# Token-major weight products in pairs of 512 columns, and attention, recurrence and latent attention in another order of work

## The reference, cut to what matters

```python
# first block, twice
h = rms_norm(x, attn_norm[i]);  proj = h @ w_in[i]              # 1024 -> 2304 (q, k, v) + 3072 (gates)
qa, ka, va, qb, kb, vb, qc, kc, vc, gates = jnp.split(proj, SPLIT_POINTS, axis=-1)
# per head: rms_norm and rope on q, k; softmax attention (full, window 128 with sinks, differential)
g = jax.nn.sigmoid(gates.reshape(B, S, N_BRANCH, D))
merged = g[:, :, 0] * (ya @ w_pa[i]) + g[:, :, 1] * (yb @ w_pb[i]) + g[:, :, 2] * (yc @ w_pc[i])
x = x + merged @ w_out[i]
u = causal_depthwise_conv(rms_norm(x, mlp_norm[i]) @ w_up[i], conv_w[i], conv_b[i])
x = x + (jax.nn.silu(gate_u) * val_u) @ w_down[i]
...
# recurrence (LRU) of the second block
gate_branch, rec = jnp.split(x @ w_in, 2, axis=-1);  u = causal conv of rec (4 taps) + conv_b
r = sigmoid(u_blocks @ w_a + b_a);  i = sigmoid(u_blocks @ w_x + b_x)
log_a = -8 * r * softplus(-lam);  a = exp(log_a)
b_in = sqrt(-expm1(2 * log_a)) * (i * u);  h_t = a_t h_{t-1} + b_in_t
return (h * gelu(gate_branch)) @ w_o
...
# latent attention (MLA) of the second block
c_q, c_kv, k_pe = jnp.split(x @ w_in, [384, 640], axis=-1)
q = rms_norm_2(c_q, q_norm_g) @ w_uq;  kv = rms_norm_2(c_kv, kv_norm_g) @ w_ukv   # rope on parts, softmax, @ w_o
...
# every MLP of the second block
return jnp.square(jax.nn.relu(x @ w1)) @ w2
```

## Time and profile before

| | us |
|---|---|
| median of 3 runs | 2251.13 |
| lowest, highest | 2250.94, 2255.55 |
| the profiled execution | 2252.48 |
| its span in the trace | 2250.7 |
| PE busy | 2151.1 (96% of the span) |
| DVE, ACT, POOL busy | 1391.1 (62%), 1097.8 (49%), 142.2 (6%) |
| share of PE's granted clock, mean | 0.989 |
| HBM read | 374.87 MB, 167 GB/s over the span |

### The profile page before, as it was taken

The page is one execution under the profiler, slowest core; times in us unless marked ns, Lnnn a source line. Parts: engine busy times, 40 slices in busy tenths (PEclk is TensorE's granted clock), DMA queues, the critical chain, the costliest instruction groups (busy, mean ns, idle before and its releaser), DMA issues.

```text
span 2250.7 us, 33710 instructions
## 1 busy us (share of the span) xinstructions
PE 2151.1 (96%) x14705; PEld 1979.4 (88%) x14711; DVE 1391.1 (62%) x1473; ACT 1097.8 (49%) x1262; POOL 142.2 (6%) x82
## 2 busy tenths in 40 slices
PE   6998999998899999999999989998999999999998
PEld 6888899898889999988999878997789989988997
DVE  4856677676567766656655685555666557465654
ACT  4475555555636554344544574443545434354443
POOL 1100010020001002300000010000000004000000
PEclk9999999999999999999999999999999999999999
DMA  7433555563245555644556545565345565545553
GB/s 234 155 103 126 171 185 184 170 203 111 80 164 173 187 186 170 199 131 158 191 189 209 176 131 169 188 202 159 122 139 186 188 205 177 175 150 170 186 188 130
DMA packets 272268, 378.10 MB, mean 168 GB/s; under 512 B 13957, under 2 KB 234362, under 8 KB 272122
## 3 DMA queue, kind: packets, MB, share of 16 engines
q1 hardware_dynamic: 271212, 374.57, 51.1%
q10 hardware_dynamic: 910, 1.38, 0.2%
HBM read 374.87 MB, written 1.05 MB: 167 GB/s over the span
## 4 chain that ended last, share of the span: by engine, by line
PE 81%; DVE 7%; ACT 4%; DMA 2%; DVEq 2%; issue 1%; SPq 1%; PEld 0%; POOL 0%; ACTq 0%; PEldq 0%; POOLq 0%
PE bank L682 51%; PE acc L682 28%; DVE slot_lo L1725 3%; PE bank L680 2%; DVEq L1720 2%; ACT slot_hi L1323 1%; DMA slot<-in_w_in 1%; DMA slot<-in_lru_w_in 1%; ACT arena L1318 1%; SPq L557 0%; PEld bank L682 0%; DVE arena L2279 0%; DVE split L1758 0%; ACT split L1351 0%; DVE arena L2064 0%
## 5 line engine op out<-in xcount | busy, mean ns | idle before, releaser
L1725 DVE TENSOR_TENSOR slot_lo<-slot,slot_hi 128x2048 fp32r<-128x2048 f32 (+1 forms) x344 | 806.9, 2350 | 422.6 <-ACT slot_hi L1323 421.4
L682 PE MATMUL bank<-split,slot_hi 128*128 128x256 f32 x5496 | 1004.3, 285 | 9.6 <-DVE slot_lo L1725 3.4
L682 PEld LDWEIGHTS bank<-split,slot_hi 128*128 128x128 f32 x5496 | 865.4, 193 | 23.4 <-issue 10.4
L1323 ACT ACTIVATE slot_hi<-slot 128x2048 fp32r<-128x2048 f32 (+1 forms) x344 | 652.9, 1902 | 280.8 <-DMA slot<-in_mlp_w 137.3
L682 PE MATMUL bank<-split,slot_lo 128*128 128x256 f32 x2748 | 779.8, 284 | 0.0
L682 PE MATMUL acc<-slot_hi,split 128*128 128x512 f32 x1904 | 610.4, 393 | 13.7 <-DVE split L2318 8.4
L682 PEld LDWEIGHTS bank<-split,slot_lo 128*128 128x128 f32 x2748 | 529.2, 193 | 0.0
L682 PEld LDWEIGHTS acc<-slot_hi,split 128*128 128x128 f32 x1904 | 359.8, 189 | 91.9 <-DVE split L2318 8.6
L682 PE MATMUL acc<-slot_lo,split 128*128 128x512 f32 x952 | 373.2, 392 | 0.0
L682 PE MATMUL bank<-slot_hi,split 128*128 128x256 f32 (+1 forms) x1616 | 306.4, 289 | 21.4 <-DVE split L1758 11.8
L1318 ACT ACTIVATE arena<-bank 128x512 f32<-128x512 f32 (+1 forms) x199 | 111.6, 573 | 388.2 <-PE bank L682 358.2
(11 more groups left out here) (195 smaller groups left out, 1036.5 us busy)
## 6 DMA issues: line engine op xcount, KB each, us to landing
slot<-in_mlp_w SPq DMA_DIRECT2D x128, 1024.0 KB, 5.4
slot<-in_ret_w_in SPq DMA_DIRECT2D x48, 1024.0 KB, 5.2
slot<-in_w_up SPq DMA_DIRECT2D x44, 1024.0 KB, 5.1
slot<-in_w_in SPq DMA_DIRECT2D x42, 1024.0 KB, 5.4
slot<-in_w_down SPq DMA_DIRECT2D x22, 1024.0 KB, 4.9
slot<-in_ret_w_o SPq DMA_DIRECT2D x16, 1024.0 KB, 4.9
slot<-in_lru_w_in SPq DMA_DIRECT2D x10, 1024.0 KB, 7.8
slot<-in_w_out SPq DMA_DIRECT2D x8, 1024.0 KB, 6.1
```

Source lines behind the costliest of these rows:

```text
L682: i = nc.tensor.matmul(o, w, m, start=start, stop=stop)
L1323: A(whi[u.r][:, 0:u.cols], raw[u.r][:, 0:u.cols], ACT.Copy).then_inc(slot_hi[u.r], 1)
L1725: TTO(wlo[u.r][:, 0:u.cols], raw[u.r][:, 0:u.cols], f32(whi[u.r][:, 0:u.cols]), ALU.subtract)\
```

## The change

Slots and products:

- Where two token-major chunks of 256 columns stood, there is now a pair: two slots, each with half of the contraction (512 rows) and 512 columns, and two banks, one for each token tile. A pair is 2 x 24 matmuls of 512 columns where there were 2 x 48 of 256. There are 23 pairs: 4 in each layer's q, k, v (`PAIRS` takes the place of `CHUNKS`), the head of the up projection in each layer, the heads of the four MLPs and of the recurrence, and four in each retention. Chunk 5 stays single.
- In a head, `rows_come` issues the matmuls that need only the high part of the activations for a half of the features, 8 for each half and token tile, then those that need the low part. Before, `token_rows` waited for the low part first, and the three products of each tile stood together.

Layers of the first block:

- Gate chunks 0, 1 and 2 stand ahead of the transposes of q and k (before: 0 and 1), gate 3 behind them, gate 4 between the first two groups of scores, then 5.
- The values of a head wait for that head's copy of the probabilities, not for those of all heads of the group.
- DVE's `divisors(3)` stands ahead of `scores(4)`.
- `yt` 3 is transposed one branch earlier, and its low part made one earlier.

Recurrence: chunk 2 is done first and chunks 0 and 1 are brought back behind it; gates 0 to 5, chunk 5, gates 6 to 9; the groups are six and four feature tiles; the sigmoid is written as a tanh of half the argument, its halves folded into the constants; POOL's product and ACT's square move to DVE; each group's output has its own `lyT` tile.

Latent attention: the layer norm rows are issued behind `mukv`; ACT copies the first two banks ahead of the high parts of `muq` 0 and 1; DVE makes the low part of `mukv` 1 ahead of the first `exchanged` of q.

The rows of the other norms (`gain`, `layer_norm`) are issued in the middle of the stages, at s = 5 or 8, or behind the first output slot of a retention.

```diff
-CHUNKS = (6, 7, 0, 1, 3, 5, 4, 2, 8)
+PAIRS = ((6, 7), (0, 1), (3, 4), (5,), (2, 8))
+LRU_ORDER = (2, 0, 1, 3, 4)
+LRU_GROUPS = (slice(0, 6), slice(6, 10))
...
+            def rows_come(u, o, name, tt, i, end):
+
+                w = [part[u.r][:, :].rearrange("p (k n) -> p k n", n=512) for part in (whi, wlo)]
+                h = [part[:, 4 * i:4 * i + 4, tt * P:(tt + 1) * P] for part in hT]
+                pe.wait_ge(V["hi_out"], his[name, (tt, i)].uses + 1)
+                for k in range(4):
+                    mm(o[:, :], h[0][:, k, :], w[0][:, k, :], (i, k) == (0, 0), False)
+                    mm(o[:, :], h[0][:, k, :], w[1][:, k, :], False, False)
+                evacuated(pe, banks[name, (tt, i)])
+                for k in range(4):
+                    mm(o[:, :], h[1][:, k, :], w[0][:, k, :], False, (i, k) == (1, 3), end if (i, k) == (1, 3) else None)
...
+            def token_pair(us, bs):
+
+                opened = [open_bank(b) for b in bs]
+                for i, u in enumerate(us):
+                    arrived(u)
+                    for tt in range(TT):
+                        half_rows(u, opened[tt][0], tt, i, opened[tt][1])
+                    freed(u)
...
-                    in_sbuf(f"pt{L}", js)
                     u = banks[f"y{L}", g]
                     o, end = open_bank(u)
                     nh = len(js)
-                    for tt in range(TT):
-                        for j in range(nh):
+                    for j in range(nh):
+                        in_sbuf(f"pt{L}", [js[j]])
+                        for tt in range(TT):
...
-                gates([0, 1])
+                gates([0, 1, 2])
                 wait(V["roped_ab"], L + 1)
                 wait(V["roped_c"], L + 1)
                 for i in range(7):
                     transposes(banks[f"qk{L}", i], qkr, 2 * i, 2 if i < 6 else 1)
-                gates([2])
+                gates([3])
                 in_sbuf(f"qk{L}", range(7))
                 softmax_scores(f"s{L}", range(4), pairs)
-                gates([3])
+                gates([4])
                 softmax_scores(f"s{L}", range(4, 8), pairs)
-                gates([4, 5])
+                gates([5])
...
-                    if b == 2:
+                    if b == 1:
                         wait(V["yc_ready"], L + 1)
                         transposes(banks[f"yt{L}", 3], y1, 6)
...
+                divisors(3)
                 scores(4)
                 gates_ahead(9)
-                divisors(3)
...
-            layer_norm(4)
             for i in range(4):
 
                 u, w = slots["muq", i], I["mla_w_uq_2"][0]
...
+            layer_norm(4)
...
+            half_tanh(range(6))
+            decays(0)
+            copies("lw", 5, lgt[:, 0:2, :])
+            weights.ahead(slots["lw", 5])
+            half_tanh(range(6, 10))
```

462 lines of the change are left out of this document (251 added, 211 removed).

## The result

| | before | after |
|---|---|---|
| median of the runs, us | 2252.46 (4 runs, 2250.94 to 2255.55) | 2222.84 (4 runs, 2221.36 to 2224.44) |
| ratio to before | | 0.9863, interval 0.9849 to 0.9877 |
| span of the profiled execution, us | 2250.7 | 2219.5 |
| PE busy, us | 2151.1 | 2141.7 |
| PE idle in the span, us | 99.6 | 77.8 |

A forecast was written before the change was run, and what follows sets the result against it. PE, busy 96% of the span, was taken as the bound. Layers 17.4, retentions 4.8, MLP heads 5.6, recurrence 2.0 and latent attention 8.9 sum to 38.7 us: 2252.5 to 2213.8 profiled, 2212.5 median; range 2198 to 2233.

The forecast's parts named there:

- The three new waits in the attention: Attention, each layer: PE waits taken as 3 us at the eighth score, 2 at gate 9, 2.5 at the last group.
- Width: Token-major slots: 24 matmuls of 512 columns save 0.58 us per pair of slots, 8.1 us for 14 pairs.
- The heads: Start of a stage's products: waiting only for the high part of the activations saves PE 0.7 to 0.8 us.
- The latent stage: Latent attention: moved norm rows and ACT copies, an earlier low part and its head save 8.9 us, bounds 7.5 and 9.5.
- The recurrence: Recurrence stage: lru_y comes 1.5 us earlier; gain 2 us, bounds -1 and 4.
- rival 4: q, k, v and retention pairs: bank copies queued behind late transfers stop PE; 28 us slower, 2279 us; chance 0.05.
- the wait for the rope: q, k, v: gate 2 fills PE's wait before the transposes; gains 7.0 us in layer 0, 8.2 in layer 1.
- the clock behind the new waits: Attention: half clock after the new idles costs 2 us more in each layer, bounds 0 and 6; 1.7 back in layer 1.
- the branches: Third branch's transpose one branch earlier removes waits for its low part and the merged sum: 2.4 and 2.6 us.
- the values: Attention: five groups' first value products wait for one copy, not four, gaining 3.0 us in each layer.
- 3 (2220.5, width saves nothing): Token-major pairs: 512 columns take as long as two of 256, saving 0 instead of 8.1 us; 2220.5; chance 0.08.
- Rival 1: Attention: gates 5 and 6 wait, the clock costs more, 10 us for both layers; recurrence gives -1; 2225.5 us; chance 0.24.

The follow-up runs named there:

- the narrow pairs: The changed kernel with every 512-column matmul of a pair issued as two of 256 columns; span 2230.3 us, ratio 0.9912 to the kernel before.
- the merged high part first: The changed kernel with ACT making the first merged high part ahead of a late slot's high part; span 2215.1 us, ratio 0.9834 to the kernel before.
- the tanh: The kernel with the three edits, with the gates' sigmoid taken as a tanh of half the argument; span 2183.9 us, ratio 0.9702 to the kernel before.
- the three edits: The changed kernel with divisors(3) between mask adds and maxima, divisors(4) earlier, gate 4's copy and the first merged high part ahead of slots' high parts; span 2195.4 us.
- the divisors between: The changed kernel with divisors(3) between scores(4)'s mask adds and maxima, and divisors(4) ahead of a slot's low part; span 2204.0 us, ratio 0.9783.
- the low part first: The changed kernel with the wait for the activations' low part ahead of a head's first matmul, as before; span 2230.7 us, ratio 0.9883.

## Why the prediction was right, and where it was off

**Right, in mechanism and size.** The three new waits in the attention: 2.77 us at the eighth score (2.7 worked out, 2.8 if the rows are added up without rounding, 3 taken), 2.20 at gate 9 (2.0), 2.42 and 2.41 at the last group (2.5); each ended by the instruction named. Width, 0.57 us a pair in the retentions (0.58), shown by the narrow pairs. The heads, 0.97 to 0.34 us, so 0.63 where 0.8 was taken; the four MLPs gave 4.5 us together for 5.6. The latent stage, 9.1 us (8.9). The recurrence, 2.7 (2.0): its last wait fell by 5.3 us, 1.2 came back at the slots ahead of the gates (a wait of 2.91 for a low part where 1.69 stood), and the rest is not settled. What rival 4 describes, work for PE queued on ACT behind a late transfer, did occur at a small price: at the merged sum, a place that it didn't name, and at one bank copy of a q, k, v pair in each layer, a place that it did (next paragraph).

**Luck in the number.** The median, 2222.84 us, lies in the range of 2198 to 2233, but 10 us above the 2212.5 of the forecast. Without the 2.3 us that retention 0 gave over its term it would be further off. Some 1.7 of them are a stretch of half clock that stood in the profile of before behind two waits of 0.74 and 0.73 us; the same two waits have none behind them in the second retention of that profile.

**Off: the wait for the rope.** The step "with four pairs shorter by 0.58 the wait is 6.1 us wide" failed in layer 0. PE ends the pairs at 74.4 us against 74.9, 0.5 us sooner and not 2.3: what each pair saves goes into waits, 1.29 us at 63.38 among them. The row puts that one down to nothing ("issue"), but PE's last pair opens two banks at once, and ACT's copy out of the second ends at 63.3:

```profile
60.78 0.22 ACT L1444 ACTIVATE stat<-stat 128x16 f32<-128x16 f32 x1 [5.27 <-DVE stat L1932]
60.91 1.90 ACT L1360 ACTIVATE slot_hi<-slot 128x2048 fp32r<-128x2048 f32 x1
62.71 1.06 ACT L1467 ACTIVATE arena<-bank 128x512 f32<-128x512 f32 x2
```

So it is a bank copy behind a norm's step and a slot's high part. DVE comes late to its share of that step, since two low parts (7.67 us) stand ahead of it and the first of them belongs to a slot that lands at 49.6. Layer 1 has 0.55 us of the same at 479.68. The forecast had named PE waits for bank copies in pairs as a sign of being wrong; here they are, though small. PE is then the last to come to the transposes (92.06; DVE's rope ends at 90.6), they start later than the forecast's 90.0, and the gain up to the first scores is 5.8 us, not 7.0 (101.22 with a gate chunk more behind it, against 101.24).

**Off: the clock behind the new waits.** The term "2 more in each layer" was too small, by 1.6 and 1.7 us. In layer 0's attention PE was busy 13.6 us at half clock, so 6.8 are lost, where before it was 3.2: 3.6 more. In layer 1 it is 6.8 for 4.8: 2.0 more, where the forecast had 2.0 less the 1.7 of the stretch at 547.6. It is the size that failed, not the mechanism. A slot behind such a wait took 7.4, 7.5, 7.7 and 7.3 us for 5.75 to 5.78, and this makes a wait of 2.2 us cost 3.7. It is not a fixed price: in the run with narrow pairs the same 2.20 us at gate 9 of layer 0 have no half clock behind them.

**Off: the branches.** The step "removes the waits for its low part and, with what follows, for the merged sum: 2.4 and 2.6" failed in its second half. The 1.41 us went; PE then came sooner to the merged sum, waited 1.72 us for it instead of 0.76, and ran the slot behind at half clock. Result in layer 0: from the end of the attention to the end of the first output slot 0.7 us are lost, not 2.4 gained. (The recorded waits add up to 2.2 and 2.4, not to the 2.4 and 2.6 of the sum.) Rope, attention and branches together make the miss of layer 0: 1.2, 0.7 and 3.1 us of 5.1 (in the attention the clock took 1.6 more than its term, and the rest 0.9 less). The run with the merged high part first shows the cause: ACT's list puts a slot that lands late ahead of it. I had moved PE and DVE in that phase and not walked ACT's list past the high part of the slot.

**Off: the values.** 3.0 us a layer were counted for the copies, and the run with that part undone shows 0. Some 1.1 us a layer of it are taken by the waits at gate 9 and at the last group, which end at a time that DVE and ACT set: the forecast treated gains and new waits as a sum, and they are a chain. The rest is met by the clock: the kernel with this part has 10.3 us more at half clock than the kernel with it undone, and the cause of that is open.

Of the rivals, 3 (2220.5, width saves nothing) and 1 (2225.5) are nearest to the 2222.8 measured. The narrow pairs rule out 3. Rival 1 is right in kind, the layers took back more, but by another route: neither gate 5 nor 6 waits, the recurrence did not lose, and in layer 0 it was the branches that took the most.

Of the rules of the Trainium skill: the one named ahead of the result (TensorE: Matmul & The Clock Gate, "Back-to-back issue gap") has the isolated cost at 2.5 ns above the columns; the retentions with 256 and 512 columns, 2.3 us apart for 4 x 48 merged matmuls, show 12 ns a merged pair. ScalarE: Activation LUTs, section "What ACT_TABLE_LOAD costs", counts 2.66 us for a switch, 1.28 of them the load and the rest a drain. Here the load takes 1.28 us as it says, but ACT's busy time in layer 0 falls by 13.2 us from the changed kernel to the one with the tanh (123.59 to 110.40) with ten loads fewer, 1.3 each, and around a load there is no gap (ACT in the changed kernel, a slot's high part, the load, the copy): no run of this kernel shows the drain.

```profile
109.91 1.90 ACT L1360 ACTIVATE slot_hi<-slot 128x2048 fp32r<-128x2048 f32 x1
111.82 1.28 ACT L1355 ACT_TABLE_LOAD   x1
113.11 0.60 ACT L1355 ACTIVATE arena<-bank 128x512 f32<-128x512 f32 x1
```

## What to carry to other kernels

When a wait is removed, ask which instruction the bound engine meets next and what time *other* engines set for it; gains ahead of such a point are not a sum but are taken, in part, out of the next wait. In an engine's list the work that the bound engine waits for should stand ahead of work that prepares something three steps on, above all where that preparation waits for a transfer: three edits of a few lines to these lists gave 24 us of span here, where the whole change gave 31. An order that puts part of an operation first, the part that frees a buffer or feeds the slow engine, beat both whole orders.

## What the runs showed of the hardware

- The half clock stands beside idle gaps of PE as short as 0.96 us (layer 1 at 513.7 in the run with the three edits, a stretch of 6.8 us), and beside two of 0.74 and 0.73 us in a row (the kernel before, 1025.5, a stretch of 3.4). It stayed away after others of the same length (layer 0 of the run with the three edits at 111.83) and after longer ones: 3.12 us at 1247.9 and 3.00 at 1309.4 with the divisors between. So the length of a gap alone does not tell its price. In these traces the stretches are 3.4, 6.8 or 10.2 us long, apart from that at the end of the run.
- Executions of one kernel differ by it: of the kernel with the three edits, those of 2189.2 and 2195.4 us of span had a mean granted clock of 0.998 and 0.995, of that with the low part first, those of 2222.5 and 2230.7 had 0.992 and 0.987.
- Removing waits gave more than their sum: with the divisors between, 3.9 us of waits less in each layer (2.20 and 2.42, less the new 0.74) and 8.0 and 9.8 us of time. The half clock in these stages fell by 10.2 and 13.6 us, which is 5.1 and 6.8 us of time and, with the waits, slightly more than the difference.
- The total at half clock within the span was 47.6 us in the run before, 50.2 after the change, 22.8 with the three edits and 12.4 with the tanh.
